# The rows of an expert's token table in another order, in a two-block transformer with 64 experts

## The reference, cut to what matters

```python
def hier_moe(h, w_group, w_expert, w1, w3, w2):
    ...
    gates = g_w[:, None] * top_p / jnp.sum(top_p, axis=-1, keepdims=True)
    expert_id = g_sel[:, None] * MOE_PER_GROUP + top_i      # 2 experts of 64 for each of 512 tokens
    ...
    def expert_block(args):
        xb, e = args
        hid = jax.nn.silu(xb @ w1[e]) * (xb @ w3[e])        # w1, w3: 1024 x 256
        return hid @ w2[e]                                   # w2: 256 x 1024
    ...
    out = jnp.zeros((n_tok + 1, dm), ys.dtype).at[slot_tok].add(ys)[:n_tok]
```

```
 8 15 20 25 16 16 19  9 14 12 18 13 19 22 18 18
21 14 26 20 14 10 13 16  6 13 20 12 12 11 11 21
20 13 27 13 23 14 16 16 16 15 13  8 20 16 22 20
14 13 16 13 18 15 12 13 17 15 28 15 12 18 13 18
```

## Time and profile before

| what | us |
|---|---|
| median of three runs | 1604.18 |
| lowest and highest of them | 1602.31, 1608.41 |
| the profiled execution, as timed | 1606.86 |
| its span in the trace | 1605.1 |

### The profile page before, as it was taken

One profiled execution on the slowest core, in us unless ns is written; L12 is line 12 of the kernel. 1 busy time (PEld: TensorE's weight loads), 2 busy tenths in 40 slices (PEclk: granted clock), 3 DMA queues, 4 the chain that ended last, 5 costly groups with the idle time before them and its releaser, 6 DMA issues. The chain is left out here.

```text
span 1605.1 us, 22033 instructions
## 1 busy us (share of the span) xinstructions
PE 1407.7 (88%) x8290; PEld 995.9 (62%) x8290; DVE 417.4 (26%) x1057; ACT 491.7 (31%) x1083; POOL 629.1 (39%) x726
## 2 busy tenths in 40 slices
PE   7999999898999999998999978669988887888781
PEld 6688876676888888886677857434444444444440
DVE  3003047713111102212245041532211111111114
ACT  4326357733322222223464312212211111111111
POOL 4334545443444444443458433123332222222222
PEclk9999999998999999999899989779999999999996
DMA  3322311031332233321313314749999999999964
GB/s 126 119 97 101 109 38 42 29 105 53 105 105 79 79 105 106 105 79 54 118 53 106 105 32 186 301 166 392 393 400 403 407 402 397 391 386 392 389 265 161
DMA packets 91463, 300.17 MB, mean 187 GB/s; under 512 B 12980, under 2 KB 35664, under 8 KB 66816
## 3 DMA queue, kind: packets, MB, share of 16 engines
q1 hardware_dynamic: 83136, 283.37, 47.0%
q0 software_dynamic: 8160, 15.75, 2.8%
q10 hardware_dynamic: 96, 0.08, 0.0%
HBM read 294.94 MB, written 12.62 MB: 192 GB/s over the span
## 5 line engine op out<-in xcount | busy, mean ns | idle before, releaser
L471 POOL TENSOR_TENSOR wring_halves<-wring,wring_halves 128x512 fp32r<-128x512 f32 (+1 forms) x275 | 357.8, 1305 | 409.5 <-ACT wring_halves L466 408.8
L466 ACT CAST wring_halves<-wring 128x512 fp32r<-128x512 f32 (+1 forms) x275 | 168.4, 618 | 465.3 <-PE ps L1035 442.0
L1033 PE MATMUL ps<-wring_halves,big_halves 128*128 128x512 f32 x612 | 244.2, 399 | 16.9 <-POOL wring_halves L471 13.5
L1033 PE MATMUL ps<-hT_halves,wring_halves 128*128 128x512 f32 (+1 forms) x496 | 195.2, 393 | 5.0 <-DVE big_halves L1553 5.0
L1034 PE MATMUL ps<-big_halves,wring_halves 128*128 128x512 f32 (+1 forms) x496 | 194.8, 393 | 0.0
L1035 PE MATMUL ps<-hT_halves,wring_halves 128*128 128x512 f32 (+1 forms) x496 | 194.5, 392 | 0.0
L2209 POOL DMA_INDIRECT y_dram<-xn,sidx x64 | 57.1, 891 | 325.6 <-DVE xn L1969 283.6
L1034 PE MATMUL ps<-wring_halves,hT_halves 128*128 128x512 f32 x436 | 173.1, 397 | 0.0
L1035 PE MATMUL ps<-wring_halves,hT_halves 128*128 128x512 f32 x436 | 172.4, 395 | 0.0
L1460 PE MATMUL ps<-big,arena 128*32 128x256 f32 x1024 | 124.6, 395 | 36.7 <-DMA big<-in_moe_w_dram 36.2
L1033 PEld LDWEIGHTS ps<-wring_halves,big_halves 128*128 128x128 f32 x612 | 117.1, 191 | 45.3 <-POOL wring_halves L471 16.6
(11 more groups left out here) (328 smaller groups left out, 1833.0 us busy)
## 6 DMA issues: line engine op xcount, KB each, us to landing
big<-in_moe_w_dram SPq DMA_DIRECT2D x86, 1024.0 KB, 23.7
wring<-in_moe_w_dram SPq DMA_DIRECT2D x66, 1024.0 KB, 26.3
wring<-in_ffn_w_in_dram SPq DMA_DIRECT2D x22, 1024.0 KB, 6.6
hT<-in_moe_w_dram SPq DMA_DIRECT2D x20, 1024.0 KB, 22.9
wring<-in_fox_w_in_dram SPq DMA_DIRECT2D x7, 2048.0 KB, 8.2
wring<-in_gla_w_in_dram SPq DMA_DIRECT2D x6, 2048.0 KB, 7.9
mkv<-in_moe_w_dram SPq DMA_DIRECT2D x10, 1024.0 KB, 30.1
xn<-in_moe_w_dram SPq DMA_DIRECT2D x10, 1024.0 KB, 30.2
```

Of the source, the lines that this page charges most:

```text
L466: act.copy(hi, src).then_inc(s_hi, 1)
L471: pool.tensor_tensor(lo, src, hi, ALU.subtract).then_inc(s_lo, 1)
L1033: pe.matmul(out, lhs[1], rhs[0], start=start, stop=False)
```

## The change

Only the 32 numbers in `iow` change. Before, column c holds c, so that rank r takes row r. After, the iota walks 16 pairs: column 2s holds s and column 2s+1 holds 16+s, so that rank s takes row 2s and rank 16+s takes row 2s+1. An expert with 16 assignments fills rows 0, 2, 4, ..., 30 instead of rows 0 to 15; one with 20 fills the even rows and rows 1, 3, 5 and 7. Both tables come out of the same `iow`, so gather and scatter use the same places. The number of instructions, their sizes, the waits and the rows moved stay as they were.

```diff
             me.inc(pool.iota(ioe, pattern=[[1, EXPERTS]], channel_multiplier=0, **small))
             me.inc(pool.iota(iob, pattern=[[1, NB]], channel_multiplier=0, **small))
-            me.inc(pool.iota(iow, pattern=[[1, C]], channel_multiplier=0, **small))
+            me.inc(pool.iota(iow.rearrange("p (s a) -> p s a", a=2), pattern=[[1, C // 2], [C // 2, 2]], channel_multiplier=0, **small))
             me.link(pool.iota(ovc, pattern=[[1, SPILL]], channel_multiplier=0, **small))
```

## The result

| | us |
|---|---|
| before, median of 4 runs | 1605.93 (1602.31 to 1608.41) |
| after, median of 4 runs | 1587.12 (1586.56 to 1588.45) |
| ratio, 95% interval | 0.9886 (0.9863 to 0.9909) |
| span of the profiled execution, before and after | 1605.1, 1584.9 |

The change makes the kernel 18.8 us faster, 1.1%. The prediction was 1591.6 us in a range from 1587 to 1599: the direction and the place were right, the size was too small by a third.

What follows compares the result with a forecast made beforehand. The prediction took the experts' stage to be bound by the slowest DMA engine: 78 rows fewer at 0.159 us gave 12.4 us, plus 0.16 us in the first gather, so 1604.2 - 12.6 = 1591.6 us, range 1587 to 1599.

Steps and rivals of the forecast that it cites:

- The slowest of the sixteen engines is the bound: Experts' loop, late: three views said the slowest DMA engine, not all sixteen together, sets the pace of 8.44 us an expert.
- the tail of rows 7: End of the weights: DMA share falls to 0.45, 0.43, 0.40, read as about ten engines done 15 to 20 us early.
- The long issues of SP: Weight loads: SP's issue of 1 MB grows from 0.33 to 2.32 or 7.09 us, read as one engine's ring being full.
- DMA engine i serves rows 2i and 2i+1: Gathers and scatters: two neighbouring rows per engine, so engine 0 carries 128 gathered rows, falling to 88 after.
- Dealt modulo 16: Rival on gathers and scatters: rows 0 and 16 share engine 0, making the change slower, 1616 us; chance 0.04.
- Dealt four to an engine: Rival on gathers and scatters: four rows per engine, about 158 rows saved on engine 0, 1579 us; chance 0.05.
- The iota at nothing: Router: the iota with another stride costs nothing, at worst 0.2 us on POOL, covered by the 23 us before its use.
- The price of a row: Experts' loop: each row removed from engine 0 saves 0.159 us, its packet's time in the first gather.
- the sum: Experts' loop: 78 rows fewer on engine 0 at 0.159 us each, 12.4 us saved.
- the upper bound of 0.194 us: Experts' loop: time per row from the busy stage, small packets and waits included; 15.1 us saved for 78 rows.
- What is late next: Experts' loop after the change: engine 0 still slowest, pace 8.25 us, above 8.06 us for all engines together.
- Rival (a): Experts' loop: the sixteen engines together are the bound, or second rows hide behind weight packets; no change, 1604.2 us; chance 0.06.

Runs made afterwards that it cites:

- one_heavy: Kernel before with ranks 0 and 1 kept together on engine 0 and the other ranks spread one to an engine as far as they go; 1592.2 us, ratio 0.9914.
- odd_reversed: Changed kernel with the order of engines reversed for experts of odd number, by eight small DVE instructions; 1585.5 us, beside 1584.5 us for the changed kernel.
- pairs_apart: Kernel before with the same rows per engine, but ranks 2i and 2i+1 in rows 4i and 4i+1, spread over all 32 partitions; 1601.6 us, ratio 0.9963.
- fours_apart: Kernel before with the same rows per engine, but ranks 4i to 4i+3 in rows 8i to 8i+3, groups of four still full; 1609.6 us, ratio 1.0032.

## Why the prediction was right, and where it fell short

- **The slowest of the sixteen engines is the bound.** Right for the kernel before. one_heavy shows it: one engine with the old load costs 12.3 us. Of the three views given for it, the tail of rows 7 carries. The long issues of SP do not: in odd_reversed, with even engines, SP's issues of gate and up weights from 1160 to 1520 us have the same median, 2.24 us (below, in ns) against 2.26 us before.

```profile
L647 SPq DMA_DIRECT2D big<-in_moe_w_dram x42: 332/2237/6867, 1172.4 to 1487.0; - x42
```

- **DMA engine i serves rows 2i and 2i+1.** Right. The four tables that keep or change the load by this rule (one_heavy, pairs_apart, fours_apart, odd_reversed) behave by it, most plainly odd_reversed with its even end. Dealt modulo 16, fours_apart would put two rows on engines 0 to 3 and 8 to 11 where the old table puts one, and be slower; it stays at 501.7 us. Dealt four to an engine, pairs_apart would have the load of the new table, and its 20.5 us; it gains 5.9 us. The first gather of the kernel after was to show eight packets nearly together. From 1057.80 to 1058.00 us it reads

```profile
DMA packets 14, 0.02 MB, mean 123 GB/s; under 512 B 8, under 2 KB 8, under 8 KB 14
```

  Six of 4 KB start in those 0.2 us, the other two later. Eight engines at work, but not in step; four with two rows each, one behind the other, it no longer is.
- **The iota at nothing.** Right in effect, not in size: it took 323 ns in place of 180, under the cover named.

```profile
L2176 POOL IOTA arena<- x1: 323/323/323, 1022.3 to 1022.3; 128x32 f32 x1
```

- **The price of a row, 0.159 us from its packet.** This is the term that was mis-sized. For a scattered row it holds (0.17 us). For the load of one engine it holds (0.158 us in one_heavy). What the sum left at nothing is the weight packets: they became shorter, from 0.332 to 0.324 us in the mean, which for 1392 of them is about 11 us. An estimate for the slowest engine shows the two together: 1392 x 0.332 + 246 x 0.159 = 501 us before (measured 502.0) and 1392 x 0.324 + 168 x 0.159 = 478 us after (481.5), with the mean packet of all engines put in for its own. one_heavy comes to 493 (493.8), pairs_apart to 497 (496.1). The longer packets go with gathers, and filling whole groups of four partitions made them longer still. The sum was 12.4 us; the stretch says 20.5. Of these, 5.9 us come from the full groups alone (pairs_apart), and 14.6 us from there to the new table, of which 12.3 are what one engine with 246 rows costs. The 2.3 us left between the two go with pairs_apart and one_heavy differing in that six engines instead of one are heavy; by the table, the six have 4 us more in packets and 2 us less in the rest. I had the upper bound of 0.194 us from the busy stage in hand, which gives 15.1 us, and put its excess down to small packets and waits of the row itself. I did not price the weight packets.
- **What is late next.** Wrong. The pace was to be 8.25 us with engine 0 still the slowest, above the 8.06 us of all engines together. It is 8.09 us, at that common rate, and odd_reversed, 1.8 us shorter with 38 rows less on the slowest engine, shows that engine 0 hardly counts any more. Rival (a) was wrong as the description of the kernel before and is nearly right as that of the kernel after.
- **Rates.** Late in the stage 409 GB/s against near 400 forecast, for the same reason. The tail of 16 us came as forecast (17 us).
- **The rule on traffic with device memory** (the Trainium skill, DMA: Bandwidth & Descriptors, Specifications): 358 GB/s for a core is exceeded here still more clearly, with 410 GB/s and, gathers cut, 421 GB/s. No other core was at work.

The effect of the groups, 5.9 us, is one that a page bears on and that I did not weigh. The Trainium skill, SBUF — State Buffer, Door 1: The DMA port swizzle, lets four neighbouring partitions share one of the ports through which DMAs reach SBUF. By it, 16 rows in partitions 0 to 15 use four ports, and in the even partitions up to 30 eight. The trace agrees as far as fours_apart (501.7 us) and pairs_apart (496.1 us) go, in the gathers only; that ports are the cause is inferred from the grouping, no run here shows a port itself, and neighbouring DMA engines would explain it as well.

## What to carry to other kernels

Where a stage is bound by DMAs that run on all engines evenly, look for the small transfers beside them that do not: partly filled tables, padded blocks, skipped rows. The end of the stage tells it in one look, since a DMA share that falls to a fraction and stays there means that some engines have more to do; how such a table is dealt out can be read from the first transfer in an idle stretch. Price such a transfer not by its own packets alone but also by what it does to the packets beside it, for which a run without it is the short way. Long issues on the queue of a steady stream are no sign of uneven engines: they look the same where the engines are even.

## What the runs showed of the hardware

- An indirect DMA of 32 rows puts rows 2i and 2i+1 on DMA engine i, and a skipped row still costs a packet of 4 bytes.
- With gathers of 4 KB rows into SBUF beside them, the 8 KB weight packets take 0.332 us in the mean over the stretch instead of 0.315 us (0.324 us with the rows spread); from 1300 to 1360 us the rate goes from 421 to 398 GB/s (410). Scatters of as many rows add little: with gathers running, cutting them leaves the mean at 0.331 us, and 421 GB/s is with them running.
- Four filled rows in an aligned group of four partitions (two neighbouring DMA engines) cost 5.9 us more over the stretch than two; whether the groups lie side by side or apart makes no difference.
- With 246 down to 0 rows on the DMA engines beside even weights, the packets of an engine in the mean leave 15.9 us of the stretch free; with 130 down to 114 rows, 2.4 us.
